# Adding the attention mask by matmul into PSUM instead of by VectorE

## The reference

```
_, idx = lax.top_k(score, k_sel)
kg = k[b_idx, idx]
vg = v[b_idx, idx]
att = jnp.einsum('btngd,btknd->btngk', qg, kg).astype(jnp.float32) * scale
att = jnp.where(valid[:, :, None, None, :], att, -jnp.inf)
p = jax.nn.softmax(att, axis=-1).astype(dt_)
o = jnp.einsum('btngk,btknd->btngd', p, vg)
```

## Time and profile before

| | |
|---|---|
| runs of the kernel before, us | 1388.03, 1400.82, 1386.03; median 1388.03 |
| the profiled execution's own time, us | 1388.03 |
| its span in the profile, us | 1386.0 |
| TensorE matmul busy | 95% of the span |
| VectorE, ScalarE, GpSimd busy | 66%, 48%, 32% |
| mean granted clock of TensorE | 0.972 of full speed |

### The profile page before, as it was taken

The page is one execution under the profiler, slowest core; times in us unless marked ns, Lnnn a source line. Parts: engine busy times, 40 slices in busy tenths (PEclk is TensorE's granted clock), DMA queues, the critical chain, the costliest instruction groups (busy, mean ns, idle before and its releaser), DMA issues.

```text
span 1386.0 us, 22043 instructions
## 1 busy us (share of the span) xinstructions
PE 1318.5 (95%) x8246; PEld 1144.5 (83%) x8246; DVE 911.4 (66%) x1421; ACT 671.0 (48%) x1128; POOL 443.3 (32%) x233
## 2 busy tenths in 40 slices
PE   5998999999978999999999999999999988999998
PEld 5785899997856799999788888799999956899998
DVE  6676533334788543333672766569999987599997
ACT  5535544445436544444445444345545533455553
POOL 4113544443530544444435322130000002354443
PEclk9769999999999999999899999999999999999999
DMA  8012566664301566665357533254454523266663
GB/s 250 1 61 91 186 191 186 188 191 144 108 31 59 165 203 183 187 190 161 116 167 223 157 92 91 63 142 139 147 151 129 163 71 105 83 194 191 193 191 107
DMA packets 170428, 197.13 MB, mean 142 GB/s; under 512 B 14077, under 2 KB 135421, under 8 KB 170365
## 3 DMA queue, kind: packets, MB, share of 16 engines
q1 hardware_dynamic: 169147, 192.07, 45.8%
q10 hardware_dynamic: 1218, 4.21, 0.8%
HBM read 195.20 MB, written 1.05 MB: 142 GB/s over the span
## 4 chain that ended last, share of the span: by engine, by line
PE 68%; DVE 23%; issue 4%; ACT 3%; DMA 1%; POOL 1%; DVEq 0%; SPq 0%; ACTq 0%
PE acc L627 22%; PE wk L575 11%; PE wk L577 11%; PE wk L576 11%; DVE LO L2357 4%; DVE arena L2286 2%; PE acc L575 1%; PE wk L1016 1%; PE acc L1042 1%; PE acc L576 1%; PE acc L577 1%; PE wk L696 1%; DVE arena L1787 1%; DVE LO L446 1%; PE wk L896 1%
## 5 line engine op out<-in xcount | busy, mean ns | idle before, releaser
L446 POOL TENSOR_TENSOR LO<-raw,HI 128x1024 fp32r<-128x1024 f32 (+3 forms) x164 | 392.5, 2399 | 842.0 <-ACT HI L1261 841.8
L1261 ACT ACTIVATE HI<-raw 128x1024 fp32r<-128x1024 f32 (+3 forms) x382 | 364.5, 996 | 151.7 <-PE acc L627 69.5
L575 PE MATMUL wk<-XH,HI 128*128 128x256 f32 x1296 | 371.8, 287 | 19.1 <-DVE XL L1983 8.8
L576 PE MATMUL wk<-XL,HI 128*128 128x256 f32 x1296 | 368.6, 284 | 0.0
L577 PE MATMUL wk<-XH,LO 128*128 128x256 f32 x1296 | 368.5, 284 | 0.0
L446 DVE TENSOR_TENSOR LO<-raw,HI 128x1024 fp32r<-128x1024 f32 (+3 forms) x164 | 205.5, 1255 | 171.4 <-ACT HI L1261 171.0
L575 PEld LDWEIGHTS wk<-XH,HI 128*128 128x128 f32 x1296 | 250.5, 193 | 24.9 <-DVE XL L1983 9.8
L576 PEld LDWEIGHTS wk<-XL,HI 128*128 128x128 f32 x1296 | 250.5, 193 | 1.9
L577 PEld LDWEIGHTS wk<-XH,LO 128*128 128x128 f32 x1296 | 250.4, 193 | 0.0
L627 PE MATMUL acc<-HI,HH 128*128 128x512 f32 x424 | 131.9, 392 | 3.8 <-DVE HL L2329 3.1
L627 PE MATMUL acc<-LO,HH 128*128 128x512 f32 x424 | 131.1, 390 | 0.0
(11 more groups left out here) (350 smaller groups left out, 1980.7 us busy)
## 6 DMA issues: line engine op xcount, KB each, us to landing
raw<-in_mlp_w SPq DMA_DIRECT2D x128, 512.0 KB, 4.2
raw<-in_w_in SPq DMA_DIRECT2D x100, 512.0 KB, 3.9
raw<-in_w_up SPq DMA_DIRECT2D x44, 512.0 KB, 3.9
raw<-in_w_down SPq DMA_DIRECT2D x44, 256.0 KB, 3.1
raw<-in_att_w_in SPq DMA_DIRECT2D x16, 512.0 KB, 4.4
raw<-in_w_ssd_proj SPq DMA_DIRECT2D x16, 512.0 KB, 3.6
raw<-in_att_w_out SPq DMA_DIRECT2D x8, 512.0 KB, 4.4
raw<-in_w_out SPq DMA_DIRECT2D x8, 512.0 KB, 4.2
```

The source lines that it names most:

```text
L446: tensor_tensor(LO[:, s, cs], raw[:, s % 2, "ab".index(part), 0:m], HI[:, s, cs].bitcast(F32), ALU.subtract).then_inc(S(f"lo_{part}"), 1)
L575: mm(o, lh, rh, start=start, stop=False, skip_group_check=skip)
L576: mm(o, lh, rl, start=False, stop=False, skip_group_check=skip)
L1261: A(HI[:, s, j * m:(j + 1) * m], raw[:, s % 2, j, 0:m], ACT.Copy).then_inc(S(f"hi_{part}"), 1)
```

## The change

The mask is now added inside PSUM. For each head TensorE first multiplies the bfloat16 identity with the rows of `keep`, which writes the mask into the head's part of the bank, and the score matmul then accumulates on it. VectorE's add goes, and its maximum reads the bank. ScalarE's exponential reads the bank too and writes `p1`. Three waits move with it: the scores of jobs 4 and later wait for the exponentials (`e1_ready`) of the job that used the bank before, since these read it last; the scores of jobs 0 to 3 wait for `keep_ready`; and the wait for `p1`'s old transposes moves from VectorE to ScalarE.

```diff
 # scores1, TensorE
                 if n >= 4:
-                    pe.wait_ge(S("s1_read"), n - 3)
+                    pe.wait_ge(S("e1_ready"), n - 3)
+                else:
+                    pe.wait_ge(S("keep_ready"), 1 + tb)
                 keep_busy(wk[:, n % 4, :], 2)
                 for b in range(nh):
 ...
-                    last = mm(o, qT1[hs, hd // 2, tb * P:(tb + 1) * P], kT1[hs, hd // 4, 0:K], start=True, stop=True)
+                    mm(o, id_bf[:, :], keep[:, tb, 0:K], start=True, stop=False, skip_group_check=True)
+                    last = mm(o, qT1[hs, hd // 2, tb * P:(tb + 1) * P], kT1[hs, hd // 4, 0:K], start=False, stop=True,
+                              skip_group_check=True)
 # exps1, ScalarE
                 act.wait_ge(S("m1_ready"), n + 1)
+                if n >= 3:
+                    act.wait_ge(S("pT1_psum"), n - 2)
 ...
-                    last = A(p1[:, n % 3, ks], p1[:, n % 3, ks], ACT.Exp, bias=small[:, n % 2, 1, b:b + 1], scale=HD ** -0.5,
+                    last = A(p1[:, n % 3, ks], wk[:, n % 4, ks], ACT.Exp, bias=small[:, n % 2, 1, b:b + 1], scale=HD ** -0.5,
 # largest1, VectorE
                 dve.wait_ge(S("s1_psum"), n + 1)
-                if n >= 3:
-                    dve.wait_ge(S("pT1_psum"), n - 2)
-                s = p1[:, n % 3, :].rearrange("p (a k) -> p a k", a=nh)
-                TT(s, wk[:, n % 4, :].rearrange("p (a k) -> p a k", a=nh),
-                   keep[:, tb, 0:K].unsqueeze(1).to_broadcast([P, nh, K]), ALU.add).then_inc(S("s1_read"), 1)
-                dve.wait_ge(S("s1_read"), n + 1)
-                link(V.tensor_reduce(small[:, n % 2, 0, 0:nh], s, AXIS.X, ALU.max))
+                link(V.tensor_reduce(small[:, n % 2, 0, 0:nh], wk[:, n % 4, :].rearrange("p (a k) -> p a k", a=nh),
+                                     AXIS.X, ALU.max))
```

More of the change, by code:

```diff
@@ L2117, in largest1 @@
                 tb, h0, nh = JOBS1[n]
-                K = P * (tb + 1)
                 dve.wait_ge(S("s1_psum"), n + 1)
-                if n >= 3:
-                    dve.wait_ge(S("pT1_psum"), n - 2)
-                s = p1[:, n % 3, :].rearrange("p (a k) -> p a k", a=nh)
-                TT(s, wk[:, n % 4, :].rearrange("p (a k) -> p a k", a=nh),
-                   keep[:, tb, 0:K].unsqueeze(1).to_broadcast([P, nh, K]), ALU.add).then_inc(S("s1_read"), 1)
-                dve.wait_ge(S("s1_read"), n + 1)
-                link(V.tensor_reduce(small[:, n % 2, 0, 0:nh], s, AXIS.X, ALU.max))
+                link(V.tensor_reduce(small[:, n % 2, 0, 0:nh], wk[:, n % 4, :].rearrange("p (a k) -> p a k", a=nh),
+                                     AXIS.X, ALU.max))
                 TS(small[:, n % 2, 1, 0:nh], small[:, n % 2, 0, 0:nh], -HD ** -0.5, None, ALU.mult)\
```

## The result

The changed kernel takes 1403.06 us in the median of 20 runs (1396.68 to 1432.06), the kernel before 1388.03 us in 20 runs beside it (1379.73 to 1401.05). The ratio is 1.0124, with a 95% interval from 1.0102 to 1.0145: slower by 1.2%, or 17 us, where 0.6% or 7.9 us was forecast and the range ended at 1401.0. The ratio goes by the usual executions alone and leaves out slower ones such as that of 1432.06 us, whose mean granted clock was 0.945. The two medians lie 15.0 us apart and the two lowest times 16.95 us.

What follows compares the result with a forecast made beforehand. TensorE was taken to bound the stage's middle, VectorE only its end. TensorE's added 8.6 us less 0.7 us at the tail gave +7.9 us on 1388.0, so 1395.9 us, range from just below 1390.0 to 1401.

Steps and rivals of the forecast that it cites:

- TensorE bounds the stage's middle, VectorE its end: Whole stage: TensorE sets the 3.20 us rounds; removing VectorE's adds gains only 0.7 us, at the tail.
- An identity of 128 columns streams for 0.06 us, one of 256 for 0.11: Added mask matmuls on TensorE: streaming of 16 x 0.06 + 16 x 0.11, 2.7 us in all.
- A round trip into the narrow shape costs 0.30 us, and there are 3 and 1 more of them a job: Between identities and scores on TensorE: array shape changes add 5.9 us over jobs 0 to 3 and 4 to 11.
- The rival of the free change of shape: TensorE's masks and scores: only streaming is paid, +2.0 us, 1390.0 us; chance 0.12.
- that of the dearer one: Short identities on TensorE: weights load in the open, some 0.10 us each, +11.1 us, 1399.1 us; chance 0.10.
- Waits and readers moved at no cost: VectorE and ScalarE reading PSUM and the moved semaphore waits in the stage: costed at nothing.
- The clock holds: TensorE in the stage: granted clock stays at 1.00, with no term for a fall in the sum.
- the sum +8.6 - 0.7: Whole stage: TensorE's added matmuls and shape changes less VectorE's gain at the tail, +7.9 us; chance 0.60.
- this fall as a rival: TensorE's clock falls to 0.50 in jobs 0 to 3: +6.2 us, 1402.1 us if in all four; chance 0.16.

Runs made afterwards that it cites:

- the kernel with one mask a job: Changed kernel, but each job's mask is one 512-column matmul ahead of all its scores; stage 44.0 us, ratio 1.0043, again 1.0030.
- the kernel of one shape: Changed kernel, but each mask matmul uses the score's 64 partitions, leaving out the other 64 queries' mask; stage 54.2 us, ratio 0.9991.
- TensorE's part alone: Kernel before, VectorE's add kept, plus an identity-times-zeros matmul ahead of each head's score; stage 59.6 us, ratio 1.0106.

## Why the prediction was wrong

- **TensorE bounds the stage's middle, VectorE its end.** Right. Rounds stayed at 3.20 us without VectorE's adds, and the end gained 0.7 us of the 0.7 forecast. In the changed kernel's round VectorE was busy for 2.31 of 3.71 us, where some 2.5 were forecast.
- **An identity of 128 columns streams for 0.06 us, one of 256 for 0.11.** Right in one piece: a mask of 512 columns a job added 0.22 us. Behind fillers and in the scores' own shape two of 256 columns added 0.13 us and not 0.22.
- **A round trip into the narrow shape costs 0.30 us, and there are 3 and 1 more of them a job.** Right in the sum. Jobs took 2.74 us for 2.76 forecast, rounds 3.71 for 3.70. How a round's added 0.51 us divides is less sure than the sum had it: 0.22 for the columns and 0.29 for the round trip by the kernel with one mask a job, 0.13 and 0.38 by the kernel of one shape. The rival of the free change of shape falls by these rows and by the kernel of one shape; that of the dearer one, which would have made jobs about 3.2 us and rounds 3.9, falls too. The Trainium skill says in "TensorEngine Tiling (Array Packing)", section Key Properties, that a change of the tiling mode drains TensorE; these rows agree with it.
- **Waits and readers moved at no cost.** Right: with them and without the masks the stage took the 41.4 us of the forecast, and TensorE's part alone has the slowdown.
- **The clock holds.** Wrong, and this is the step that failed: the sum +8.6 - 0.7 has no term for TensorE's clock, which stood only among the rivals. At full clock the stage would have taken 42.1 + 8.6 - 0.7 = 50.0 us; that is an estimate, which the job of 2.74 us and the round of 3.71 us bear out, and no run of the changed kernel showed it whole. It took 58.9 and 60.2, with a granted clock of 0.50 for 20.5 and 23.9 us. The fall costs 8.9 to 10.2 us, more than all the added instructions.

The prediction had this fall as a rival, with the place where it begins right: within jobs 0 to 3. The 1402.1 us that it gave for that rival are the nearest of its figures to the 1403.06 measured. But it gave it a chance of 0.16 and a price of 6.2 us at most, and both were too small. The chance rested on one stretch late in the stage, busy 3.43 of 5.00 us, that kept its clock. The prediction set it against what it had worked out itself, that the streaming part of a job falls from 1.32 of 1.62 us to 1.56 of 2.76, and gave the stretch more weight. The profile's busy time couldn't warn, since it is full in either case: 20.07 of 20.40 us at half clock in TensorE's part alone.

The price was too small for two reasons. The fall was taken to end with job 3, and it went on through the first round of tb = 1, which took 6.77 us for 3.71, and into the next. And only the 1.56 us of streaming in a job were taken to double, while a whole job took 4.63 us at half clock for 2.74, which is 1.89 more: the passages between the shapes grow too.

What stays open: how often the fall ahead of the stage occurs in each kernel, which property of the jobs makes the clock fall, and why it stays low as long as it does. The streaming part of a job doesn't settle the last point: in the kernel of one shape it is by estimate 1.56 us of the 1.86 that a job would take at full clock (1.62 + 4 x 0.06), no smaller a part than before, and yet a fall from ahead of the stage lasted through all four short jobs and into the rounds.

## What to carry to other kernels

Handing an add to TensorE as a matmul with an identity is nearly free if it is laid out in one piece ahead of the narrower matmuls, and best in the place of a filler; put between matmuls of another array shape, each one paid 0.29 to 0.38 us here for going out and in. When TensorE is kept at full clock by fillers, don't take a full busy row as a sign that the clock will hold: price the fall as a case of its own, from a job at either clock, and read the granted clock of the stage in more than one profile. Here it cost more than the work that was added. And cut the comparison of two profiles at the stage that changed: the part ahead of it, the same code in every kernel here, took from 398.4 to 412.4 us.

## What the runs showed of the hardware

- A fall of the clock in the interleaved stage lasted 20.5 us in three profiles and 23.9 in one, although TensorE was noted busy for nearly all of it. With six fillers in place of two in jobs 0 to 3 a fall from ahead of the stage was over 3.1 us into it; in the kernel of one shape such a fall lasted 23.9 us.
- A change between the 128\*128 and the 64\*128 shape and back cost 0.29 us at full clock against one mask a job, 0.38 us against the kernel of one shape, and 0.33 us at half clock. In one shape a matmul in float32 started 0.12 us after one of 256 columns in bfloat16.
- A job with masks a head took 2.74 us at full clock and 4.63 us at half, a round 3.71 and 6.77.
- The exponential of 256 columns took 0.465 us on average from PSUM in the changed kernel; before, from SBUF, it took 0.50.
